# Gaps in SBUF that set where the split moving operands begin against the weights, in a one-core float32 transformer kernel

## The chip, the cores and the metric

One core of one Trainium2 chip runs the whole program in one launch. The metric is device time in microseconds, lower is better. Three runs of the kernel before took 3042.85, 3035.99 and 3043.49 us, median 3042.85.

## The reference, cut to what matters

Two stacks of two layers each work on an activation of 512 tokens by 1024 channels, in float32. The first stack is

```python
x = x + 0.5 * swiglu(rmsnorm(x), w_ffn1_in, w_ffn1_out)     # 1024 -> 2*2816 -> 1024
x = x + mixing_sublayer(rmsnorm(x), ...)                    # retention and forgetting attention, gated
x = x + 0.5 * swiglu(rmsnorm(x), w_ffn2_in, w_ffn2_out)
```

and the second stack runs a hybrid layer twice: one projection of the normed input, four small mixers (window attention, gated convolution, latent attention, stick-breaking attention), group norms, a gate and an output projection. Nearly all arithmetic is a product of the activation with a weight matrix.

## The kernel before

The activation lies channel-major in SBUF as `x`, eight slices of 128 channels by 512 tokens. A float32 product is made from three float32r matmuls: both operands are split into a high part rounded to float32r and the low rest, and the kernel forms high*high + high*low + low*high. The weights come from HBM as 460 panels of 128 x 1024 floats, eight units of 128 columns each. SyncE loads a panel into `raw` (two slots), ScalarE writes its high part to `wh` (L1068), VectorE its low part to `wl` (L1461); `wh` and `wl` have four slots each. The helper `mm3` (L462 to L467) issues for one unit

1. L465: weights `wh` unit, moving high operand (128 x 512 floats),
2. L466: the same weights, moving low operand,
3. L467: weights `wl` unit, moving high operand.

While one matmul streams its moving operand, the weights of the next one are loaded. The moving pairs are `xh`/`xl` (input of every projection of the normed activation, 2384 units), `uh`/`ul` (hidden activation of the feed-forward, 704 units), `mh`/`ml` (128 units), `yrh`/`yrl` and `yfh`/`yfl` (64 each), `ygh`/`ygl` (128) and `cqh`/`cql`, `ckh`/`ckl` (24 in all). In `token_major` (L573 to L575) the roles are exchanged: `xh`/`xl` are the weights, by 128 tokens, and `wh`/`wl` are moving.

Each engine runs its own program, in order, and they meet by semaphores. Of the feed-forward, `ffn_in` runs over 22 pairs of panels with `xh`/`xl` moving, and `ffn_out` over 22 panels with `uh`/`ul` moving; there are four such feed-forwards. In the mixing layer come `token_major` twice, four, then sixteen, then eight panels with `xh`/`xl` between the attention heads, then the merge with `yrh`, `yfh` and `xh` in turn, and the output projection with `mh`/`ml`. The hybrid layer has 25 panels with `xh`/`xl`, one of which (L916 to L919, called the `k_rope` panel here) takes its eight weight blocks not at units of 128 columns but at column 512 + 48*k of the slot, k from 0 to 7.

SBUF tensors are placed one behind the other in the order in which they are declared; each begins at the next multiple of 32 bytes of the partition, and `x` begins at byte 1152. Tensors of a stage that has been closed share their bytes with those of the next. A unit of 128 floats is 512 bytes and a token row of 512 floats is 2048 bytes, so every unit of `wh` and `wl`, and every slice of a moving tensor, has the start of its tensor modulo 512. From the sizes in the code, before the change:

| tensors | start modulo 512 | less the weights' 192 |
| --- | --- | --- |
| `wl`, `wh` | 192 | |
| `xh`, `xl` | 128 | 448 |
| `uh`, `ul`, `yrh`, `yrl`, `yfh`, `yfl`, `mh`, `ml` | 256 | 64 |
| `ygh`, `ygl` | 384 | 192 |
| `cqh`, `cql`, `ckh`, `ckl` | 288 | 96 |
| `ffh` / `ffl` (weights here, one block each 288 bytes) | 224 / 192 | |

The last column is called the distance below: start of the moving operand less start of the weights that are loaded beside it, modulo 512. In `token_major` it is 192 - 128 = 64. In the `k_rope` panel the weights start at 192 + 192*k, so the distance of `xh` to block k is 448 - 192*k: 448, 256, 64, 384, 192, 0, 320, 128 for k = 0 to 7. L465 and L466 of block k stream while weights of the same block are loaded, and L467 while the first of block k + 1 is.

Of the kernel before, what the change touches and what calls it, by code (L numbers as in the profile page):

```python
# [14 lines left out]
F32 = mybir.dt.float32  # L15
# [7 lines left out]
P = 128  # L23
# [120 lines left out]
def build(nc, stream, x_in, vec, const, decay, rope, ff_w, pos, out):  # L144
    ctx = ExitStack()
    with ctx:
        def sb(name, shape, dt=F32, stack=ctx):
            return stack.enter_context(nc.sbuf_tensor(name, shape, dt))

        def sem(name):  # L150
            return ctx.enter_context(nc.semaphore(name))

# [1 line left out]


        x = sb("x", [P, KD, S])
        xh = sb("xh", [P, KD, S], F32R)
        xl = sb("xl", [P, KD, S], F32R)
        sq = sb("sq", [P, S])
# [3 lines left out]
        std_col = sb("std_col", [P, TT])  # L163
        rstd_col = sb("rstd_col", [P, TT])
        raw = sb("raw", [P, RAW_SLOTS, PANEL])
        wl = sb("wl", [P, SLOTS, PANEL], F32R)
        wh = sb("wh", [P, SLOTS, PANEL], F32R)
        vecs = sb("vecs", [P, N_VEC])
# [11 lines left out]


        ffn = ExitStack()
        uh = sb("uh", [P, KF, S], F32R, ffn)
        ul = sb("ul", [P, KF, S], F32R, ffn)
        ta = sb("ta", [P, S], F32, ffn)
# [6 lines left out]
        whole = sb("whole", [P, S], F32, ffn)  # L192
        ffn.close()
        mix = ExitStack()
        yrh = sb("yrh", [P, RH, S], F32R, mix)
        yrl = sb("yrl", [P, RH, S], F32R, mix)
        yfh = sb("yfh", [P, FH // 2, S], F32R, mix)
# [38 lines left out]
        fz, fa = fq[:, 0, :], fq[:, 1, :]  # L236
        heads.close()
        merge_mem = ExitStack()
        mh = sb("mh", [P, KD, S], F32R, merge_mem)
        ml = sb("ml", [P, KD, S], F32R, merge_mem)  # L240
        sr = sb("sr", [P, S], F32, merge_mem)
# [24 lines left out]
        cu = sb("cu", [P, CONV_K - 1 + S], F32, qkv_mem)  # L266
        cy = sb("cy", [P, S], F32, qkv_mem)
        lat_mem = ExitStack()
        cqh = sb("cqh", [P, 2, S], F32R, lat_mem)
        cql = sb("cql", [P, 2, S], F32R, lat_mem)  # L270
        ckh = sb("ckh", [P, S], F32R, lat_mem)
# [27 lines left out]
        out_mem = ExitStack()  # L299
        z = sb("z", [P, KD, S], F32, out_mem)  # L300
        yg = sb("yg", [P, 2, S], F32, out_mem)
        gstd = sb("gstd", [P, 4, TT], F32, out_mem)
        ginv = sb("ginv", [P, 4, TT], F32, out_mem)
        ygh = sb("ygh", [P, KD, S], F32R, out_mem)
        ygl = sb("ygl", [P, KD, S], F32R, out_mem)
        out_mem.close()
        hyb.close()


        raw_in = [sem(f"raw_in{i}") for i in range(RAW_SLOTS)]  # L310
        split_hi, split_lo = sem("split_hi_act"), sem("split_lo_dve")
        panel_done = sem("panel_done")
        x_part = [sem(f"x_part{i}") for i in range(X_PARTS)]
        vec_in, const_in, pos_in = sem("vec_in"), sem("const_in"), sem("pos_in")
# [1992 lines left out]
```

## Time and profile before

| | |
| --- | --- |
| median of three runs | 3042.85 us (3035.99 to 3043.49) |
| time of the profiled execution | 3036.15 us |
| its span, first to last instruction | 3034.4 us |
| TensorE matmul busy | 2953.1 us, 97% of the span |
| weight loads busy | 2378.1 us, 78% |
| VectorE, ScalarE busy | 1446.1 us (48%), 998.1 us (33%) |
| mean granted TensorE clock | 0.989 of full |
| matmuls | 13442 |

Matmuls overlap: a row of the timeline gives 0.39 us for one, while the next starts some 0.23 us behind it. The cost of a matmul in a dense stretch is thus the distance from its start to the next start (called the pitch below), and the duration in the rows is longer than that by the time which the pipeline takes. The page has 40 slices with TensorE at 8 or 9 tenths in each.

### The profile page before, as it was taken

The numbers are of one execution on the slowest core, as the hardware profiler recorded it, in microseconds if no ns is written. First come the engines' busy times: TensorE is split into PE (matmuls) and PEld (weight loads), VectorE is DVE, ScalarE is ACT, GpSimd is POOL, SyncE is SP. The second block draws the span as 40 slices with busy tenths as digits, with TensorE's granted clock in tenths as the row PEclk, the third lists the DMA queues.
The fourth block names the chain that finished last, engine by engine and source line by source line (L and its number), as shares of the span: only waits on it lengthen the run. The fifth ranks groups of instructions, "written<-read, shape, count | busy, mean of one in ns | idle before, by whom it ended". The sixth has DMA issues, their size and how long they took to land.

```text
span 3034.4 us, 36777 instructions
## 1 busy us (share of the span) xinstructions
PE 2953.1 (97%) x13442; PEld 2378.1 (78%) x13442; DVE 1446.1 (48%) x2087; ACT 998.1 (33%) x1546; POOL 0.2 (0%) x4
## 2 busy tenths in 40 slices
PE   8999999999999999999999999999998999999996
PEld 6888887778888887888887778888887877777775
DVE  6443345555544425444255554544435445455555
ACT  3222223333322322222123233332223345434453
POOL 0000000000000000000000000000000000000000
PEclk9999999999999999999999999999999999999998
DMA  4323232212233232323232212323332121122111
GB/s 139 91 89 103 90 115 78 62 56 83 90 97 97 90 104 84 97 91 101 92 116 77 70 55 76 97 84 96 97 98 83 63 69 42 49 84 70 43 42 56
DMA packets 69368, 251.67 MB, mean 83 GB/s; under 512 B 7696, under 2 KB 7824, under 8 KB 69008
## 3 DMA queue, kind: packets, MB, share of 16 engines
q1 hardware_dynamic: 68400, 246.46, 25.8%
q10 hardware_dynamic: 864, 3.79, 0.3%
q8 instruction: 69, 1.13, 0.1%
q14 instruction: 35, 0.29, 0.0%
HBM read 248.13 MB, written 2.10 MB: 82 GB/s over the span
## 4 chain that ended last, share of the span: by engine, by line
PE 93%; DVE 4%; ACT 2%; issue 1%; DMA 0%; DVEq 0%; SPq 0%; ACTq 0%
PE bank L465 26%; PE bank L467 26%; PE bank L466 26%; PE bank L573 1%; PE bank L575 1%; PE bank L574 1%; PE bank L628 1%; PE bank L638 1%; PE bank L818 1%; PE bank L829 1%; PE bank L695 1%; PE bank L804 1%; PE bank L748 1%; PE bank L775 1%; PE bank L760 1%
## 5 line engine op out<-in xcount | busy, mean ns | idle before, releaser
L465 PE MATMUL bank<-xh,wh 128*128 128x512 f32 x2384 | 956.5, 401 | 16.0 <-DVE start_d L2071 9.5
L466 PE MATMUL bank<-xl,wh 128*128 128x512 f32 x2384 | 945.4, 397 | 0.0
L467 PE MATMUL bank<-xh,wl 128*128 128x512 f32 x2384 | 945.0, 396 | 0.0
L1461 DVE TENSOR_TENSOR wl<-raw,wh 128x1024 fp32r<-128x1024 f32 x460 | 561.2, 1221 | 303.6 <-ACT wh L1068 302.9
L1068 ACT ACTIVATE wh<-raw 128x1024 fp32r<-128x1024 f32 x460 | 483.4, 1052 | 398.3 <-PE bank L467 251.9
L465 PEld LDWEIGHTS bank<-xh,wh 128*128 128x128 f32 x2384 | 450.3, 189 | 127.2 <-issue 18.7
L467 PEld LDWEIGHTS bank<-xh,wl 128*128 128x128 f32 x2384 | 449.9, 189 | 109.0
L466 PEld LDWEIGHTS bank<-xl,wh 128*128 128x128 f32 x2384 | 450.3, 189 | 106.5 <-issue 1.9
L1509 DVE TENSOR_TENSOR ta<-bank,rstd 128x512 f32<-128x512 f32 x88 | 60.9, 692 | 463.3 <-PE bank L467 460.7
L467 PE MATMUL bank<-uh,wl 128*128 (+1 forms) x704 | 277.4, 394 | 0.0
L466 PE MATMUL bank<-ul,wh 128*128 (+1 forms) x704 | 276.0, 392 | 0.0
L465 PE MATMUL bank<-uh,wh 128*128 (+1 forms) x704 | 273.2, 388 | 0.0
L1090 ACT ACTIVATE sa<-ta 128x512 f32<-128x512 f32 x88 | 55.8, 634 | 659.8 <-DVE ta L1509 659.7
L466 PEld LDWEIGHTS bank<-ul,wh 128*128 128x128 f32 x704 | 132.2, 188 | 30.9
L465 PEld LDWEIGHTS bank<-uh,wh 128*128 128x128 f32 x704 | 132.2, 188 | 29.6
L467 PEld LDWEIGHTS bank<-uh,wl 128*128 128x128 f32 x704 | 132.4, 188 | 26.3
L573 PE MATMUL bank<-wh,xh 128*128 128x512 f32 (+1 forms) x192 | 75.0, 391 | 6.9 <-DVE xl L1477 6.9
L575 PE MATMUL bank<-wl,xh 128*128 128x512 f32 (+1 forms) x192 | 73.0, 380 | 0.0
L574 PE MATMUL bank<-wh,xl 128*128 128x512 f32 (+1 forms) x192 | 72.7, 379 | 0.0
L1521 DVE TENSOR_TENSOR u<-sa,tb 128x512 f32<-128x512 f32 x88 | 60.9, 692 | 17.8 <-ACT sa L1090 17.8
L465 PE MATMUL bank<-ygh,wh 128*128 128x512 f32 x128 | 53.7, 420 | 7.3 <-DVE ygl L2025 7.3
L1524 DVE TENSOR_TENSOR ul<-u,uh 128x512 f32 (+1 forms) x88 | 60.3, 685 | 0.0
(355 smaller groups left out, 2832.6 us busy)
## 6 DMA issues: line engine op xcount, KB each, us to landing
raw<-stream SPq DMA_DIRECT2D x460, 512.0 KB, 3.5
x<-x_t SPq DMA_DIRECT2D x4, 512.0 KB, 8.1
dec<-decay ACTq DMA_DIRECT2D x2, 1024.0 KB, 6.3
out<-x SPq DMA_DIRECT2D x8, 256.0 KB, 2.0
rp<-rope ACTq DMA_DIRECT2D x2, 512.0 KB, 7.6
cst<-const SPq DMA_DIRECT2D x1, 708.5 KB, 10.8
ffraw<-ff_w ACTq DMA_DIRECT2D x2, 316.0 KB, 9.8
posi<-pos SPq DMA_DIRECT2D x1, 256.0 KB, 10.4
```

The source lines that it names most:

```text
L465: pe.matmul(o, wh[:, s, c], rhs_h, start=first, stop=False)
L466: pe.matmul(o, wh[:, s, c], rhs_l, start=False, stop=False)
L467: return pe.matmul(o, wl[:, s, c], rhs_h, start=False, stop=last)
L573: pe.matmul(o, xh[:, k, tok], wh[:, slot, w], start=k == 0, stop=False)
L574: pe.matmul(o, xl[:, k, tok], wh[:, slot, w], start=False, stop=False)
L575: last = pe.matmul(o, xh[:, k, tok], wl[:, slot, w], start=False, stop=k == KD - 1)
L1068: act.activation(wh[:, at.slot, :], raw[:, at.raw, :], ACT.Copy).then_inc(split_hi, 1)
L1090: act.activation(sa[:], ta[:], ACT.Silu).then_inc(fin_act.sem, 1)
L1461: dve.tensor_tensor(wl[:, at.slot, :], raw[:, at.raw, :], wh[:, at.slot, :].bitcast(F32), ALU.subtract).then_inc(split_lo, 1)
L1509: dve.tensor_tensor(dst, src, rstd[:], ALU.mult).then_inc(st.sem, 1)
L1521: dve.tensor_tensor(u32[:], sa[:], tb[:], ALU.mult).then_inc(fin.sem, 1)
L1524: dve.tensor_tensor(ul[:, j, :], u32[:], uh[:, j, :].bitcast(F32), ALU.subtract)\
```

## The change

A helper `gap` declares a tensor that nothing uses. Seven of them stand ahead of moving operands and of `wl`. No instruction is added, removed or reordered; only addresses differ.

```diff
+        def gap(name, size, stack=ctx):
+            sb("gap_" + name, [P, size // 4], F32, stack)
         x = sb("x", [P, KD, S])
+        gap("xh", 160)
         xh = sb("xh", [P, KD, S], F32R)
...
         raw = sb("raw", [P, RAW_SLOTS, PANEL])
+        gap("wl", 192)
         wl = sb("wl", [P, SLOTS, PANEL], F32R)
...
         ffn = ExitStack()
+        gap("uh", 192, ffn)
         uh = sb("uh", [P, KF, S], F32R, ffn)
...
         mix = ExitStack()
+        gap("yrh", 192, mix)
         yrh = sb("yrh", [P, RH, S], F32R, mix)
...
+        gap("mh", 512, merge_mem)
         mh = sb("mh", [P, KD, S], F32R, merge_mem)
...
+        gap("cqh", 160, lat_mem)
         cqh = sb("cqh", [P, 2, S], F32R, lat_mem)
...
+        gap("ygh", 64, out_mem)
         ygh = sb("ygh", [P, KD, S], F32R, out_mem)
```

By the same arithmetic `wl` and `wh` then begin at 32 modulo 512, and all of `xh`, `xl`, `uh`, `ul`, `yrh`, `yrl`, `yfh`, `yfl`, `mh`, `ml`, `cqh`, `cql`, `ckh`, `ckl`, `ygh` and `ygl` at 288. The distance is 256 for each, and 256 in `token_major` too (32 - 288 modulo 512). Before, `xh`, `uh`, `wl` and `wh` began at multiples of 64 bytes; now they begin 32 bytes past one. The tensors behind `xh` move by 160 bytes and those behind `wl` by 352, those of the mixing layer and the feed-forward by 544; `raw` goes from 192 to 352 modulo 512.

## Rows read from the trace of the kernel before

**Rows 1.** The page: engines, clock by fortieths of the span, chain of work.

```profile
PE 2953.1 (97%) x13442; PEld 2378.1 (78%) x13442; DVE 1446.1 (48%) x2087; ACT 998.1 (33%) x1546; POOL 0.2 (0%) x4
PEclk9999999999999999999999999999999999999998
PE 93%; DVE 4%; ACT 2%; issue 1%; DMA 0%; DVEq 0%; SPq 0%; ACTq 0%
```

**Rows 2.** Waits of TensorE, longest first: who waited for whom, us in total, times, longest.

```profile
PE bank L465 <- DVE start_d L2071: 9.5, 1, 9.5
PE bank L465 <- DVE ygl L2025: 7.3, 8, 2.0
PE bank L489 <- DVE ssq L1488: 7.1, 2, 4.3
```

**Rows 3.** Windows: us, busy us (instructions) of PE, PEld, DVE, ACT, POOL, clock, DMA.

```profile
439.00:687.00 248.00, 242.37 (x1209) 193.64 (x1209) 127.92 (x225) 83.21 (x179) 0.00 (x0) 0.99 0.21 66
687.00:818.00 131.00, 131.00 (x576) 106.95 (x574) 72.77 (x96) 44.41 (x58) 0.00 (x0) 1.00 0.29 93
2345.00:3034.00 689.00, 643.17 (x3147) 511.70 (x3145) 351.69 (x586) 303.57 (x542) 0.00 (x0) 0.97 0.18 57
```

**Rows 4.** Timeline of TensorE in the merge: start us, us, instruction (27, then 24 pitches).

```profile
689.62 0.39 PE L465 MATMUL bank<-yfh,wh 128*128 128x512 f32 x1
...
695.79 0.39 PE L465 MATMUL bank<-xh,wh 128*128 128x512 f32 x1
...
701.38 0.39 PE L465 MATMUL bank<-yrh,wh 128*128 128x512 f32 x1
```

**Rows 5.** Timeline of TensorE in a feed-forward: 27 pitches in `ffn_in`, 27 in `ffn_out`.

```profile
199.69 0.39 PE L465 MATMUL bank<-xh,wh 128*128 128x512 f32 x1
...
205.98 0.40 PE L465 MATMUL bank<-xh,wh 128*128 128x512 f32 x1
...
299.62 0.39 PE L467 MATMUL bank<-uh,wl 128*128 x1
...
305.80 0.39 PE L467 MATMUL bank<-uh,wl 128*128 x1
```

**Rows 6.** Groups, merge and mixing output (690 to 818 us): count, busy us, mean ns of one.

```profile
L467 PE MATMUL bank<-xh,wl 128*128 128x512 f32 x64 | 25.3, 395 | 0.0
L466 PE MATMUL bank<-xl,wh 128*128 128x512 f32 x64 | 25.3, 395 | 0.0
L465 PE MATMUL bank<-xh,wh 128*128 128x512 f32 x64 | 25.3, 395 | 0.0
L467 PE MATMUL bank<-mh,wl 128*128 128x512 f32 x64 | 25.2, 394 | 0.0
L466 PE MATMUL bank<-ml,wh 128*128 128x512 f32 x64 | 25.1, 392 | 0.0
L465 PE MATMUL bank<-mh,wh 128*128 128x512 f32 x64 | 24.8, 388 | 0.0
```

**Rows 7.** Groups in `token_major` (431 to 433 us) and gated output (2640 to 2673).

```profile
L573 PE MATMUL bank<-wh,xh 128*128 128x512 f32 x4 | 1.6, 388 | 0.0
L575 PE MATMUL bank<-wl,xh 128*128 128x512 f32 x3 | 1.2, 394 | 0.0
L574 PE MATMUL bank<-wh,xl 128*128 128x512 f32 x3 | 1.2, 392 | 0.0
...
L466 PE MATMUL bank<-ygl,wh 128*128 128x512 f32 x48 | 19.0, 396 | 0.0
```

**Rows 8.** Groups in 2431.7:2431.9, the `k_rope` panel: exactly its matmuls at distance 256.

```profile
L465 PE MATMUL bank<-xh,wh 128*128 128x512 f32 x1 | 0.4, 393 | 0.0
L466 PE MATMUL bank<-xl,wh 128*128 128x512 f32 x1 | 0.4, 393 | 0.0
L467 PE MATMUL bank<-xh,wl 128*128 128x512 f32 x1 | 0.4, 392 | 0.0
```

**Rows 9.** The same panel at distance 448 (2431.27:2431.30), then at 64 (2770.7:2770.9).

```profile
L466 PE MATMUL bank<-xl,wh 128*128 128x512 f32 x1 | 0.4, 398 | 0.0
L465 PE MATMUL bank<-xh,wh 128*128 128x512 f32 x1 | 0.4, 397 | 0.0
...
L465 PE MATMUL bank<-xh,wh 128*128 128x512 f32 x1 | 0.4, 394 | 0.0
L466 PE MATMUL bank<-xl,wh 128*128 128x512 f32 x1 | 0.4, 388 | 0.0
```

**Rows 10.** Tiles `cqh` and `ffh`: duration ns min/median/max, first and last start, forms.

```profile
L465 PE MATMUL bank<-cqh,wh x16: 394/394/403, 2407.5 to 2750.7; 128*128 128x512 f32 x16
L1844 DVE TENSOR_TENSOR cql<-cn,cqh x4: 685/688/693, 2403.6 to 2743.2; 128x512 fp32r<-128x512 f32 x4
L1040 PE MATMUL bank<-xl,ffh x16: 390/394/403, 433.7 to 1597.0; 128*128 128x512 f32 x16
```

**Rows 11.** A float32 matmul (400 to 420 us), and VectorE's low part of `u` from the page.

```profile
L496 PE MATMUL bank<-diag,cst 128*128 128x512 f32 x2 | 1.0, 590 | 0.0
...
L1524 DVE TENSOR_TENSOR ul<-u,uh 128x512 f32 (+1 forms) x88 | 60.3, 685 | 0.0
```

## The prediction, made before the change was run

> **What bounds the kernel now.** I read the page first. TensorE is busy 97% of the span, 93% of the chain of work lies on it, and its clock is granted in full but for the last slice [rows 1]. Then its waits: the longest total is 9.5 us, at the start, and the next are 7 us each [rows 2]. So what a matmul takes is what the kernel takes, nearly everywhere; the windows show where it isn't so. The merge and the mixing output have no idle time at all (131.00 of 131.00), retention and forgetting attention have 242.37 of 248.00, and only the two hybrid layers leave room, 643.17 of 689.00 [rows 3]. VectorE and ScalarE, at 48% and 33%, stand behind.
>
> **What a matmul costs, by tensor.** The timeline gives starts, and the start is what counts. In the merge, 27 matmuls of `yfh`, `yfl`, `yrh`, `yrl` take 695.79 - 689.62 = 6.17 us, 228.5 ns each, and the 24 of `xh`, `xl` that follow take 701.38 - 695.79 = 5.59 us, 232.9 ns each [rows 4]. In a feed-forward 27 of `xh`, `xl` take 6.29 us, 233.0 ns each, and 27 of `uh`, `ul` 6.18 us, 228.9 ns [rows 5]. The shape and the weights' loading are the same. Stage and load on the other engines differ between the last two, but not between the first two, which stand in one chain without a wait. What differs is which tensor is moving, and so its address: distance 64 for the cheap ones, 448 for `xh`. The durations say the same in whole ns: 388, 392, 394 in turn for `mh`, `ml`, mean 391.3, and 395 for `xh` and `xl` (395.5 by pairs of 393 and 398, which is what the timeline's 0.39 and 0.40 stand for) [rows 6]. Duration less pitch is some 162.5 ns in both, so differences of durations are differences of pitch. `token_major`, with roles exchanged and the distance 64, has 388, 394 and 392, like `mh`; `ygh` at 192 has 396, like `xh` [rows 7]. This is four sets of rows in which one number, the distance, orders the cost.
>
> **What distance 256 costs.** The change puts all these pairs at 256. One panel of the kernel before passes through 256: the `k_rope` panel, whose weight blocks step by 192 bytes. Its three matmuls at 256 last 393, 393 and 392 ns, mean 392.7 [rows 8]. Are single matmuls in passing a fair sample of a steady stretch? The same panel passes 448 with 397 and 398, where the steady value is 395.5, and 64 with 394 and 388, mean 391, where the steady value is 391.3 [rows 9]. So the panel reads within some 2 ns. I take 392.7 for distance 256: 2.8 ns less than `xh` now, 1.4 more than `uh` and its like now.
>
> **The sum, part by part.** The gap ahead of `xh` with the one ahead of `wl` (edits one and two) act on 2384 units of three matmuls, 7152. Of these 4 x 22 x 2 x 24 = 4224 lie in `ffn_in` and 384 in the merge, all on the path. Another 1344 lie between attention heads, where TensorE is busy 98% [rows 3]: I count 9 in 10, 1210. The last 1200, with the 72 of `cqh` and `ckh` (edit six), lie in the hybrid layers, where TensorE waits for heads of other engines; I count half, 636. The 384 of `ygh` (edit seven) are in a dense stretch. Together 6838 matmuls at -2.8 ns, -19.1 us.
>
> The gaps ahead of `uh`, `yrh` and `mh`, together with the move of the weights, act on 704 + 128 + 128 units, 2880 matmuls, and `token_major` has 384 of 512 columns and some 190 of 384 columns, which I count as half: 3360 matmuls, all dense, at +1.4 ns, +4.7 us. The 512 bytes ahead of `mh` change nothing modulo 512 against 0 bytes. Sum: -14.4 us.
>
> Priced at nothing: the tensors that merely move. Float32 matmuls of 512 columns take 590 - 162 = 428 ns, two passes' worth of 214, and show no surcharge that could go [rows 11]; the pairs of them in the hybrid heads move together and keep their distances. VectorE's low part of `cq`, in a tensor at 288 modulo 512 as all will be, takes 685 to 693 ns, and that of `u`, at 256 now, 685 [rows 10, 11]: up to 8 ns dearer, beside matmuls that cover it, on an engine with half its time free. `raw`, whose loads wait for nothing of this, has TensorE's 5.6 us per panel as its cover. If the cover of VectorE were gone, 460 panels at some ns each would be under 4 us.
>
> Of its own profiled time, 3036.15 us, this makes 3021.8. The four times shown of before lie at 3036, 3036, 3043 and 3043, mean 3039.6, and the same spread will stand in the runs of the other kernel. I forecast 3039.6 - 14.4, about 3025 us.
>
> **The rivals.**
>
> *Distance 256 is as good as the best seen, or better.* At distance 64 the steady mean is 391.3, so 4.2 ns off 6838 matmuls, 29 us off: 3011. Were every matmul at 388, the least that recurs [rows 6], it would be 7.5 ns off 6838 and 3.3 ns off 3360, 62 us off: 2978. For it: half a period is the place that looks safest if two readers meet, one at each end. Against it: none of the three rows at 256 is under 392. A variant of the same idea is that the surcharge goes altogether. Then a matmul costs 214 ns, half of the float32 one's 428: 19 ns off 6838 and 15 off 3360, 180 us off, 2860. Rows 8 speak plainly against it, since three in a row at that distance still pay 16; I keep it at one in twenty.
>
> *Slower: the absolute start decides as well.* Before, weights and most moving tensors begin at multiples of 64 bytes; after, all begin 32 past one. Where one of the two does so now, rows are dear: `cqh` at 288 takes 394 at the least and 403 at the most, and `xl` against `ffh`, half of whose blocks lie 32 past, 390 to 403 [rows 10]. If that is a cost of its own and not one of distance, each matmul goes to the 395.5 of `xh` now: nothing gained on `xh`, 4.2 ns lost on 3360, 14 us slower, 3054. At 398, the worst value that recurs, it is 2.5 x 6838 + 6.7 x 3360, 40 us slower, 3079. The point from which it decides is where gain and loss meet: (395.5 x 6838 + 391.3 x 3360) / 10198 = 394.1 ns, only 1.4 above what I take. What speaks against it: where the odd 32 bytes are on one side, the distance is odd too, and the change makes the distance whole again.
>
> *The change does nothing.* The cheap and the dear tensors may differ by higher bits of the address or by the order of the tensors, not by the distance modulo 512. Then 3040, unchanged. Against it, rows 9: within one panel, same tensors, the cost moves as the blocks' starts move by 192 bytes. The Trainium skill has a rule that would give this result: "SBUF — State Buffer", section "Who interferes with whom", gives TensorE two independent read ports, one for the moving operand and one for the loading of weights, and says that it never waits on anyone. By that no placement could matter, and the time would be the same; the trace does not agree, with 228.5 against 232.9 ns in one dense stretch [rows 4].
>
> **How the numbers follow.** My forecast (3012 to 3034) gets 0.42; as good as 64 or better 0.20, the surcharge gone 0.05; unchanged, or gain and loss in balance, 0.14; slower 0.19. The likeliest is 3025. The low end, 2983, takes in nearly all of the first rival; the high end, 3058, its first price of slower, and leaves out the 398 case and the 180 us case, together some 0.13, with a rest of misjudged terms. A difference of 0.3%, 9 us, is about what a measurement of this kernel can tell from none. Forecast and first rival lie under 3030.5 but for the upper part of the forecast's own range: faster 0.62; same 0.20; slower 0.18.
>
> **What would show it.** Right: in the merge and in both halves of a feed-forward the rows of `xh`, `uh`, `mh` and `ygh` become alike, with durations near 392.7 and a pitch near 230 ns, the matmul count, the waits and VectorE's rows unchanged, and the span down by some 14 us, of which the four `ffn_in` give 12. Wrong: `uh` and `mh` at 395 or more (the slower rival), all at 391 or 388 (the first), `xh` still at 395.5 with `mh` at 391.3 (the last). It would be wrong in its size, and not its sense, if passing values at 256 differ from steady ones by more than the 2 ns seen at 448.

## The result, and the profile after

| | before | after |
| --- | --- | --- |
| median of four runs | 3041.45 us (3035.99 to 3043.49) | 2999.86 us (2998.0 to 3005.1) |
| ratio, 95% interval | | 0.987 [0.9855, 0.9885] |
| span of the profiled execution | 3034.4 us | 2997.6 us |
| mean granted clock of the runs (before: thirteen later ones) | 0.986 to 0.990 | 0.981 to 0.984 |

The kernel is 1.3% faster, 41.6 us, where 14.4 had been forecast: the right sign, inside the range, and a gain three times too small. The page after, beside [rows 1]:

```profile
PE 2915.8 (97%) x13442; PEld 2386.8 (80%) x13442; DVE 1446.1 (48%) x2087; ACT 998.0 (33%) x1546; POOL 0.2 (0%) x4
PE 92%; DVE 4%; ACT 2%; issue 1%; DMA 0%; DVEq 0%; SPq 0%; ACTq 0%
```

VectorE is busy for the same 1446.1 us in the same 2087 instructions; only TensorE changed. Lines of the file are 11 further on, so L476 to L478 are what L465 to L467 were. The timeline of the merge, for [rows 4]:

```profile
675.67 0.39 PE L476 MATMUL bank<-yfh,wh 128*128 128x512 f32 x1
...
682.47 0.39 PE L476 MATMUL bank<-xh,wh 128*128 128x512 f32 x1
...
687.91 0.39 PE L476 MATMUL bank<-yrh,wh 128*128 128x512 f32 x1
```

24 matmuls of `xh` and `xl` take 5.44 us, 226.7 ns each, and the 30 from the first `yfh` row to `xh` 6.80 us, 226.7 too. Groups of three dense stretches (count, busy us, mean ns of one) say it in whole ns. They are `ffn_in` at 100 to 250 us, `ffn_out` at 300 to 375 and the mixing output at 680 to 803, beside [rows 6]:

```profile
L476 PE MATMUL bank<-xh,wh 128*128 128x512 f32 x221 | 86.0, 389 | 0.0
L477 PE MATMUL bank<-xl,wh 128*128 128x512 f32 x221 | 86.0, 389 | 0.0
L478 PE MATMUL bank<-xh,wl 128*128 128x512 f32 x221 | 86.0, 389 | 0.0
...
L476 PE MATMUL bank<-uh,wh 128*128 128x512 f32 x41 | 15.9, 389 | 0.0
...
L477 PE MATMUL bank<-ml,wh 128*128 128x512 f32 x64 | 24.9, 389 | 0.0
```

Every family is at 389 ns: 6.5 less than `xh` before, 2.3 less than `uh` and `mh` before, and 3.7 less than the 392.7 that I had taken for distance 256. Duration less 162.3 is the pitch here, 226.7 ns.

Not all of that reached the end. The windows up to the hybrid layers and behind them, of before and then of after (us, busy us of PE, PEld, DVE, ACT, POOL, then clock and DMA):

```profile
0.00:2344.00 2344.00, 2308.93 (x10294) 1865.38 (x10295) 1093.41 (x1501) 693.51 (x1003) 0.20 (x4) 1.00 0.29 91
2344.00:3034.00 690.00, 644.15 (x3148) 512.70 (x3148) 352.69 (x587) 304.57 (x544) 0.00 (x0) 0.97 0.18 57
```

```profile
0.00:2301.00 2301.00, 2266.24 (x10294) 1864.90 (x10294) 1093.38 (x1500) 693.08 (x1003) 0.20 (x4) 1.00 0.30 92
2301.00:2998.00 697.00, 649.57 (x3148) 521.85 (x3148) 352.71 (x588) 304.96 (x544) 0.00 (x0) 0.94 0.18 56
```

The same instruction, the first projection of the hybrid layers, starts at 2344 us before and 2301 after: 43 us won in the first stack. The hybrid layers take 697 us where they took 690: nothing won, 6 or 7 us lost, at a granted clock of 0.94 in place of 0.97.

### The profile page after: what moved, and what is told of

The parts are those of the page before. It is cut to its first block, busy times and chain, and to the rows that moved or that the text cites. A ratio compares the mean times of both kernels' runs of the same rounds, so it can differ in the third digit from the quotient of the medians.

```text
span 2997.6 us, 36777 instructions
## 1 busy us (share of the span) xinstructions
PE 2915.8 (97%) x13442; PEld 2386.8 (80%) x13442; DVE 1446.1 (48%) x2087; ACT 998.0 (33%) x1546; POOL 0.2 (0%) x4
## 4 chain that ended last, share of the span: by engine, by line
PE 92%; DVE 4%; ACT 2%; issue 1%; DMA 0%; DVEq 0%; SPq 0%; ACTq 0%
PE bank L476 25%; PE bank L478 25%; PE bank L477 25%; PE bank L584 1%; PE bank L585 1%; PE bank L586 1%; PE bank L639 1%; PE bank L649 1%; PE bank L829 1%; PE bank L815 1%; PE bank L840 1%; PE bank L706 1%; PE bank L759 1%; PE bank L786 1%; PE bank L771 1%
## 5 line engine op out<-in xcount | busy, mean ns | idle before, releaser
L476 PE MATMUL bank<-xh,wh 128*128 128x512 f32 x2384 | 943.8, 396 | 16.4 <-DVE start_d L2082 9.2
L478 PE MATMUL bank<-xh,wl 128*128 128x512 f32 x2384 | 932.1, 391 | 0.0
L477 PE MATMUL bank<-xl,wh 128*128 128x512 f32 x2384 | 932.0, 391 | 0.0
L476 PEld LDWEIGHTS bank<-xh,wh 128*128 128x128 f32 x2384 | 450.5, 189 | 114.5 <-issue 18.5
L478 PEld LDWEIGHTS bank<-xh,wl 128*128 128x128 f32 x2384 | 450.0, 189 | 95.1
L476 PE MATMUL bank<-uh,wh 128*128 (+1 forms) x704 | 273.9, 389 | 0.0
L478 PE MATMUL bank<-uh,wl 128*128 (+1 forms) x704 | 273.9, 389 | 0.0
L478 PEld LDWEIGHTS bank<-uh,wl 128*128 128x128 f32 x704 | 132.2, 188 | 27.6
L476 PEld LDWEIGHTS bank<-uh,wh 128*128 128x128 f32 x704 | 132.2, 188 | 27.4
L476 PE MATMUL bank<-ygh,wh 128*128 128x512 f32 x128 | 53.9, 421 | 7.0 <-DVE ygl L2036 7.0
```

The lines of the kernel that those rows point to most:

```text
L476: pe.matmul(o, wh[:, s, c], rhs_h, start=first, stop=False)
L477: pe.matmul(o, wh[:, s, c], rhs_l, start=False, stop=False)
L478: return pe.matmul(o, wl[:, s, c], rhs_h, start=False, stop=last)
```

## The experiments

The forecast's price for distance 256 was wrong, and two kernels with other gaps ask by what the pitch is set. All kernels below but the one called `dwell` start from the changed kernel and differ from it in the sizes of the gaps, and where a diff shows it in one thing more; `dwell` starts from the kernel before. Each made one run, but for `even`, `x_only` and `no_mh_gap` with four and `u_only` with ten. "Distance" is again start of the moving tensor less start of `wl` and `wh`, modulo 512. Pitches are means over the dense stretches of a family, from start to next start, gaps over 262 ns left out.

**Two scans of the distance.** One kernel tries several distances, since each family has its own gap (sizes in bytes).

```diff
-gaps: xh 160, wl 192, uh 192, yrh 192, mh 512, cqh 160, ygh 64
+scan_a: xh 416, wl 448, uh 64, yrh 256, mh 64, cqh 128, ygh 480
+scan_b: xh 192, wl 160, uh 160, yrh 480, mh 448, cqh 320, ygh 160
```

> The gaps are resized so that each family of moving tensors has a distance of its own to wl and wh: xh/xl 0, uh/ul 128, yrh/yfh 320, mh 384, ygh 160, cqh 224 (and 0 for token_major). Theory D (the distance modulo 512 sets the pitch, and 256 is the bottom of it): xh at 0 is the dearest, at 235 ns or more, the others between, and the span goes up to 3040 us or over. Rival P (the period is 256, since 448 and 192, which are 256 apart, cost the same before): xh at 0 costs what 256 does, 226.7 ns, and mh at 384 what uh at 128 does; the span is near 3000 us. Rival A (the absolute start, 32 past a multiple of 64 for both operands, gave the gain): xh, uh and mh, all still 32 past, keep 226.7 and ygh, now at a multiple of 64, does not.

> As the scan before, with the distances xh/xl 288, uh/ul 224, yrh/yfh 32, mh 480, ygh 352, cqh 416 (and 224 for token_major). Theory D: xh and uh, 32 bytes to either side of 256, stay within 2 ns of 226.7 if the optimum is broad, or go to 230 and over if it is narrow; yrh and mh, next to 0, are dear. Rival P: 32 and 288 cost the same, and so do 224 and 480. Rival A: all of xh, uh, yrh, mh at multiples of 64 while the weights are 32 past; all dear, 231 to 240.

The first ran in 3009.5 us, the second in 3050.9. Groups in `ffn_in` and `ffn_out` of the first (`xh` at 0, `uh` at 128), then of the second (288 and 224):

```profile
L476 PE MATMUL bank<-xh,wh 128*128 128x512 f32 x221 | 86.0, 389 | 0.0
...
L476 PE MATMUL bank<-uh,wh 128*128 128x512 f32 x36 | 14.2, 395 | 0.0
```

```profile
L476 PE MATMUL bank<-xh,wh 128*128 128x512 f32 x215 | 85.0, 395 | 0.0
...
L476 PE MATMUL bank<-uh,wh 128*128 128x512 f32 x28 | 11.1, 396 | 0.0
```

With the two kernels already known, this is the whole scale at steps of 32 bytes:

| distance | pitch, ns | distance | pitch, ns |
| --- | --- | --- | --- |
| 0 | 227.3 (`xh`, scan_a) | 256 | 226.7 to 227.1 (after) |
| 32 | 233.3 (`yrh`, scan_b) | 288 | 233.3 (`xh`, scan_b) |
| 64 | 228.9 (`uh`, before) | 320 | 229.0 to 230.1 (`yfh`, `yrh`, scan_a) |
| 96 | 233.9 (`cqh`, before) | 352 | 233.3 (`ygh`, scan_b) |
| 128 | 233.3 (`uh`, scan_a) | 384 | 232.4 (`mh`, scan_a) |
| 160 | 234.2 (`ygh`, scan_a) | 416 | 234.3 (`cqh`, scan_b) |
| 192 | 233.3 (`ygh`, before) | 448 | 233.3 (`xh`, before) |
| 224 | 233.3 (`uh`, scan_b) | 480 | 233.3 (`mh`, scan_b) |

The right half repeats the left, within 1.2 ns. So rival P stands: the period is 256, and distance 0 is as good as 256. It isn't that two readers should start half a period apart; being at the same place in the period is the good case. Most distances cost the same 233.3, and two places, 0 and 64 modulo 256, are better.

**The absolute start.** Both sides moved by 160 bytes, to multiples of 64.

```diff
-gap("xh", 160)
+gap("xh", 320)
...
-gap("mh", 512, merge_mem)
```

> All distances 256 as in the changed kernel, but weights and moving tensors begin at multiples of 64 bytes (wl, wh at 192 modulo 512, the moving ones at 448), as they did before the change. Theory D: 226.7 ns for every family, time as the changed kernel, 2998 to 3005 us, ratio to before 0.987. Rival A (the 32 bytes past a multiple of 64 matter): the gain is lost at least in part, pitch 229 to 233, time 3020 to 3045 us.

3002.8 us (2999.6 to 3004.0), ratio 0.9875 [0.9856, 0.9893], and 389 ns for `xh`, `uh` and `mh` alike. The absolute start, at 32 past a multiple of 64 or at one, doesn't matter at distance 256. It doesn't at 64 either: `uh` has 228.9 ns with starts of 256 against weights at 192 (before) and of 96 against 32 (`x_only`, below). Rival A, in the prediction as the slower case, has fallen.

**Steps of less than 32 bytes.** Each tensor 512 bytes longer, and read from an offset:

```diff
-        xh = sb("xh", [P, KD, S], F32R)
+        xh = sb("xh", [P, KD * S + P], F32R)[:, 4:4 + KD * S].rearrange("p (a b) -> p a b", b=S)
...
-        mh = sb("mh", [P, KD, S], F32R, merge_mem)
+        mh = sb("mh", [P, KD * S + P], F32R, merge_mem)[:, 1:1 + KD * S].rearrange("p (a b) -> p a b", b=S)
```

(`xl` and `ml` likewise, and `uh`, `ul` from element 124, which puts them at distance 240 modulo 256).

> The changed kernel with the moving tensors shifted by less than 32 bytes: xh and xl at distance 272, uh and ul at 240, mh and ml at 260. If 256 is a point on a slope, one of 272 and 240 is cheaper than 226.7 ns and the other dearer; if it is the bottom of a narrow well, both are dearer, 228 to 233.3, and 260 between; if only the 32-byte block of the address counts, 272 and 260 stay at 226.7 and 240 goes to 233.3, as 224 does.

3047.2 us. In the mixing output and merge of this kernel `mh` is at 260, `xh` at 272 and `yfh` at 256:

```profile
L476 PE MATMUL bank<-mh,wh 128*128 128x512 f32 x52 | 20.8, 401 | 0.0
...
L476 PE MATMUL bank<-xh,wh 128*128 128x512 f32 x48 | 18.9, 394 | 0.0
L478 PE MATMUL bank<-yfh,wl 128*128 128x512 f32 x31 | 12.1, 389 | 0.0
```

Four bytes beside the good place cost 11 ns more per matmul (mean 238.0 against 226.7), 16 bytes 5 ns (231.7), and `uh`, 16 bytes to the other side, 9 ns (235.8). So 256 isn't a point on a slope, and the 32-byte block of the address isn't all that counts. But the expectation, that 260 would lie between 256 and its neighbours, missed: the nearest is the dearest. Two of the three, 235.8 and 238.0, are dearer than every multiple of 32 in the table; 231.7 isn't. The weights stayed at a multiple of 32 here, so these three rows don't tell the distance from the moving tensor's own start being off a multiple of 32; moving the weights by the same 4 bytes would, and wasn't tried.

**What my price was read from.** The kernel before, own addresses, with one edit that keeps the whole `k_rope` panel at distance 256. It reads other weight columns there, and so leaves out the rope part of the keys.

```diff
-                    c = KR_AT + k * KR_W
+                    c = KR_AT + KR_W + (k % 3) * P
```

> The kernel before, with its own addresses, but in the k_rope panel the weight blocks begin at column 560, 688 or 816 of the slot in turn, which keeps all 24 matmuls of the panel at distance 256 (it reads other weight columns, so the rope part of the keys is left out in effect). This is the row that my price for 256 was read from, three matmuls long, made 24 long. Theory S (a stretch needs some ten matmuls to settle, and my three were read on the way): the first seven to twelve vary between 224 and 236 ns, then all are 226 or 227. Rival A (a matmul at 256 in the old layout really costs 230 to 231, and the changed kernel gained by its absolute addresses): the mean stays at 230 to 231 to the end of the panel. Outside the panel nothing changes, time within 8 us of before.

3041.2 us, as before. The panel begins in the second hybrid layer at 2769.27 us. Its second to sixth matmul (window 2769.67:2770.62), and then fifteen in a row from 2771.1 on:

```profile
L467 PE MATMUL bank<-xh,wl 128*128 128x512 f32 x2 | 0.8, 396 | 0.0
L466 PE MATMUL bank<-xl,wh 128*128 128x512 f32 x2 | 0.8, 394 | 0.0
L465 PE MATMUL bank<-xh,wh 128*128 128x512 f32 x1 | 0.4, 389 | 0.0
...
L466 PE MATMUL bank<-xl,wh 128*128 128x512 f32 x5 | 1.9, 389 | 0.0
L467 PE MATMUL bank<-xh,wl 128*128 128x512 f32 x5 | 1.9, 389 | 0.0
L465 PE MATMUL bank<-xh,wh 128*128 128x512 f32 x5 | 1.9, 389 | 0.0
```

One by one the durations are 394, 393, 398, 389, 395, 393 and then 389 for every matmul. The panel of the first hybrid layer gives the same seven values in the same order, and then 389. The old addresses give 389 as soon as the stretch is long enough. The same shows at the head of each dense stretch of the changed kernel: pitches of 230, 236, 229, 232, 231 and then 227, 226, 227 without end; the longest such heads are nine or ten matmuls. So a matmul's pitch depends on what ran before it, and not on its distance alone. My three matmuls at 256 [rows 8] followed others at 448, and were on the way.

**Whose weights count.** With 192 bytes between `wl` and `wh` the distance is no longer the same for the two.

```diff
-        gap("wl", 192)
         wl = sb("wl", [P, SLOTS, PANEL], F32R)
+        gap("wh", 192)
         wh = sb("wh", [P, SLOTS, PANEL], F32R)
```

(and the gaps ahead of `xh`, `mh` and `ygh` resized, for the distances that the expectation names).

> A gap of 192 bytes between wl and wh, so that the two have different distances. xh, uh, yrh: 256 to wh and 448 to wl; mh: 64 to wh, 256 to wl; ygh: 384 to wh, 64 to wl. If the distance counts to the weights that are being loaded for the next matmul, the second of each three (it streams while wl is loaded) is the odd one: for xh and uh its pitch is 231 or more and the first and the third are near 227. If the distance to the matmul's own weights counts, the third is the odd one. If only the moving operand's address counts, all three are alike. Mean of xh between 227 and 233 in either case of the first two, span 3005 to 3025 us.

3041.3 us, not the 3005 to 3025 expected. `xh` in `ffn_in`:

```profile
L478 PE MATMUL bank<-xh,wl 128*128 128x512 f32 x217 | 86.3, 397 | 0.0
L477 PE MATMUL bank<-xl,wh 128*128 128x512 f32 x217 | 85.1, 392 | 0.0
L476 PE MATMUL bank<-xh,wh 128*128 128x512 f32 x217 | 84.4, 389 | 0.0
```

The third is the odd one, so I could have read this as "own weights count". But the mean, 231.1, is that of two dear matmuls (233.3) and one cheap (226.7), not of one dear. Two more kernels were made for that. The first leaves the weights and moves the low operand (`xl`, `ul`) to 448:

> The changed kernel, but a gap of 192 bytes between xh and xl and between uh and ul, so that the low operand, which the second of each three matmuls streams, is at 448 and the high one at 256. This tells which matmul a surcharge is booked to: if to the streaming one itself, the second of three is the odd one for xh and uh, at 233 or more. If it shows one matmul later, the third is the odd one; then the kernel with wl and wh apart, where the third was the odd one, speaks of the weights that are loaded while the second streams and not of the third's own. Mean of xh 229 to 233, span 3015 to 3035 us.

```profile
L477 PE MATMUL bank<-xl,wh 128*128 128x512 f32 x219 | 85.8, 392 | 0.0
L476 PE MATMUL bank<-xh,wh 128*128 128x512 f32 x219 | 85.4, 390 | 0.0
L478 PE MATMUL bank<-xh,wl 128*128 128x512 f32 x219 | 85.2, 389 | 0.0
```

3018.7 us, as expected, but no single odd one at 233: the surcharge is spread over the three (229.2, 229.2, 228.3 for `uh`), with a mean of 228.9, which is one dear and two cheap. So the mean counts dear matmuls and the booking to one of the three says little. The second puts every moving tensor at 256 to `wl` and at 448 to `wh` (`gap("wh", 320)`):

> wh 320 bytes further from wl: every moving tensor is at 256 to wl and at 448 to wh (before, in the first such kernel, it was 448 to wl and 256 to wh, and the mean was 231.1 ns, which is two of three matmuls at 233.3 and one at 226.7). If the distance to the matmul's own weights or to the ones being loaded each makes it dear, all three of a unit are dear now: mean 233.3. If only one of the two counts, two of three are dear and the mean is 231.1.

3058.3 us; `xh` 233.0, `uh` and `mh` 233.3: all three dear. Own weights alone would make the first and the second dear, the loaded ones alone the first and the third. Together with the first kernel (own 256, loaded 448: the second of three; own 448, loaded 256: the third; and two dear in the mean) this fits a rule that a matmul is cheap only when both its own weights and the next ones lie well. Two more families of the first kernel fit it: `mh`, 64 to `wh` and 256 to `wl`, has the 228.9 of distance 64 (229.1 measured), and `ygh`, 384 and 64, has all three dear (233.3). But the rule rests on means, and two families don't fit: with the same distances in the last kernel, `cqh` settled at 231.1 and `ygh` at 232.2, which I can't explain. Nor is "own weights" told from another reading of the same rows: that a load at a bad distance is dear, and so is a matmul whose weights and the next ones begin at different places.

**Is it the loading at all?** The second of each three with half of its weights:

```diff
-                pe.matmul(o, wh[:, s, c], rhs_l, start=False, stop=False)
+                half = slice(c.start, c.start + P // 2)
+                pe.matmul(o[0:P // 2], wh[:, s, half], rhs_l, start=False, stop=False)
```

> The changed kernel with the second matmul of each three on 64 of its 128 weight columns (half of the high times low product is left out), so that one load of three reads 256 bytes instead of 512. Theory L (what is left above 213 ns, 13.3 ns, is still the price of loading weights beside the stream): the mean pitch falls by 2 to 5 ns, some matmul of the three to 220 or less. Rival F (226.7 ns is what streaming 512 float32r columns costs, loading or not): all three stay at 226.7. Rival N (the shorter load breaks the settled pattern): the mean goes up.

3018.2 us. (This kernel leaves out half of the product of high weights and low operand.) The mean goes up to 229.8 in every family (229.87 `xh`, 229.78 `uh` and `mh`), which is rival N: no pitch stays at 226.7, and in its place fifteen pitches between 224 and 236 repeat, 231, 236, 228, 233, 230, 226 and so on, the values of an unsettled head. Theory L, that the mean falls, and rival F, that nothing changes, have fallen. That it is the shorter load isn't shown, since the same edit also halves the rows that the matmul writes. It doesn't answer either how much of the 12.7 ns above 214 (half of a float32 matmul, [rows 11]) is the loading's; no settled pitch lies under 226.7, though single ones fall to 223 or 224.

**One part at a time,** with the gap of 512 bytes left out in a third kernel.

```diff
 x_only: xh 160, wl 192, cqh 160, ygh 64          (uh, yrh, yfh, mh stay at 64)
 u_only: uh 192, yrh 192                          (all else as before)
 no_mh_gap: as the change, less the 512 ahead of mh
```

> Only the gaps ahead of xh and wl (and cqh, ygh), so xh, xl, cqh, ckh and ygh are at 256, while uh, yrh, yfh and mh stay at 64. By the settled pitches of the changed kernel and the one before (xh 233.3 to 227.1, uh and its like 228.9 as before) it keeps the 37 us that xh gives in the first block and lacks 2.2 ns x 2880 = 6.3 us of the changed kernel: 3004 to 3010 us. Rival (the parts aren't additive, since TensorE's clock in the hybrid layers follows from how the work falls in time): the first block is 6 us longer than in the changed kernel, 2307 us, but the hybrid layers differ by up to 10 us either way.

> Only the gaps ahead of uh and yrh: uh, yrh, yfh and mh at 256, xh at 448 and the rest as before. Worth 2.2 ns x 2880 = 6.3 us by settled pitches, nothing by my price for 256, which had it dearer by 4 us: 3034 to 3037 us against 3045, at a median of 3041 for before. Ratio 0.997 to 0.999.

> The changed kernel without the 512 bytes ahead of mh. All distances and all starts modulo 512 are the same. Expected the same pitches, 226.7 ns for mh, and a time of 2998 to 3005 us. It gives more executions of the changed kernel's layout for the clock in the hybrid layers: by the theory that quicker matmuls leave TensorE more waiting there, the mean granted clock stays at 0.981 to 0.985 in all of them, against 0.986 to 0.990 before; if that was chance, it will show 0.986 and over in about half of them.

| | median, us | ratio to before | clock of the runs | first stack in the profiled one |
| --- | --- | --- | --- | --- |
| before | 3041.1 (13 runs) | | 0.986 to 0.990 | 2344.0 |
| x_only | 3003.9 | 0.9888 [0.9861, 0.9916] | 0.981 to 0.987 | 2309.7 |
| u_only | 3038.6 (10 runs) | 0.9999 [0.9988, 1.001] | 0.985 to 0.987 | 2338.4 |
| no_mh_gap | 3000.7 | 0.9867 [0.9847, 0.9888] | 0.981 to 0.985 | 2302.9 |

In the first stack the parts nearly add up: 34.3 from `xh`, 5.6 from `uh` and its like, 39.9 against 42.7 together (41.1 in `no_mh_gap`), each from one execution. `x_only` came out at the lower edge of the 3004 to 3010 expected. At the end of the kernel the 5.6 us of `u_only` can't be told from nothing, and my expectation of 0.997 to 0.999 missed. The windows of its profiled execution show where they stayed:

```profile
0.00:2338.00 2338.00, 2303.24 (x10294) 1865.04 (x10294) 1093.13 (x1500) 692.70 (x1003) 0.20 (x4) 1.00 0.29 91
2338.00:3041.00 703.00, 656.62 (x3148) 520.47 (x3148) 353.18 (x588) 304.90 (x545) 0.00 (x0) 0.95 0.18 56
```

Its hybrid layers have the old distances and the old matmuls of `xh`, and take 703 us instead of 690, at a clock of 0.95 instead of 0.97. (13 us is more than typical, since this execution, 3043.0 us, is among the slowest of its ten, and the profiled one of before, 3036.15, in the faster half of its kernel's.) The clock has two levels, 2.4 GHz and half of it, and the traces record how long each held. From the start of the hybrid layers to the end:

| | hybrid layers, us | of these at 1.2 GHz, us (stretches) | estimate, us |
| --- | --- | --- | --- |
| before | 690.3 | 46.9 (6) | |
| u_only | 702.8 | 70.7 (8) | 702.2 |
| x_only | 691.8 | 67.2 (8) | 692.0 |
| after | 696.3 | 80.0 (10) | 698.4 |
| even | 700.5 | 87.7 (11) | 702.2 |
| no_mh_gap | 702.0 | 91.3 (12) | 704.0 |

The estimate is worked out from these rows: the 690.3 of before, plus half of what was added at 1.2 GHz, less 8.5 us for the quicker matmuls where `xh` is at 256. (Those at full speed there went from 233.2 to 228.0 ns, 1129 of `xh`, and from 233.3 to 226.9, 342 of `ygh`, with 48 of `cqh` 7.2 ns less.) It meets all five within 2.1 us. So the hybrid layers' length in these kernels is told by the pitch and the time at half clock; why that time differs isn't. In the twelve executions of the change's layout (four of the change, four of `even`, four of `no_mh_gap`) the whole kernel's clock was 0.981 to 0.985, in the thirteen of before 0.986 to 0.990, without overlap; chance, the rival that `no_mh_gap` was to test, would hardly do that. But the ten of `u_only`, whose `xh` has the old pitch, lie across the two, at 0.985 to 0.987. Within each kernel too the longer runs are those with the lower clock: 2994.5 us at 0.985 and 3006.7 at 0.981 for `no_mh_gap`, 3033.9 at 0.990 and 3043.9 at 0.986 for before.

## Why the prediction was right or wrong

**What bounds the kernel: right.** TensorE's pitch is the kernel's time in the first stack. 5952 matmuls of `xh` there at 6.2 ns less (233.3 to 227.1, unsettled heads included) are 37 us, 3264 of the others at 2.2 ns less 7 us, together 44; 42.7 were measured in the two profiled executions.

**That distance decides: right, for a reason that was half right.** Four sets of rows ordered by one number were four samples of a function that has only a few values. The experiments confirm the number, with a period of 256 and not 512: that 448 and 192 cost the same and 256 apart was in my own rows [rows 6, 7], and I did not follow it. It would have said that 256 is like 0.

**The price for 256: wrong, the step that failed.** I took 392.7 ns from three matmuls in passing; the settled value is 389. I had asked whether passing matmuls are a fair sample, and answered with the means at 448 and 64 [rows 9]. That check couldn't find the fault. At 64 the settled state is itself a round of 388, 392, 394, and an unsettled stretch has similar values, so the two agree by chance; at 448 the alternation of 393 and 398 hid it likewise. The three rows at 256, each 3 to 4 ns above the value at which they would have settled, looked the steadiest of all. With 389 in its place, the same sum is 6.5 x 6838 + 2.3 x 3360 = 52 us, where 14.4 was forecast and 41.6 measured. That 3000 us lay inside the range is owed to the range, which took in the first rival, and not to the price.

**The sign for `uh` and its like: wrong with it.** +4.7 us was forecast; the first stack of `u_only` shows -5.6.

**The hybrid layers: wrong the other way.** I counted half of their matmuls as gained. Their matmuls at full speed did get shorter, by some 8.5 us in sum, but the layers took 6 us longer, since the clock stood at 1.2 GHz for 80.0 us in place of 46.9. I had named the clock as granted in full but for the last slice; a digit of 9 there means 90% or more, and my own row for these layers had 0.97 [rows 3]. I priced nothing for a clock that falls further. Of the 52 us, 10 are missing in the medians, and 15 between the two profiled executions (36.8 won).

**The rivals.** "As good as the best seen, or better" was the case that came: its variant with 388 for all had nearly the right price, 389. Its reason, that half a period is the safest place, was wrong, for 256 is a whole period and as good as 0. I gave it 0.20 with the sentence that none of the three rows is under 392, which was true and no argument. The surcharge did not go altogether. The slower rival, absolute starts 32 bytes past 64, was tested alone and fell. "The change does nothing" fell. The Trainium skill, "SBUF — State Buffer", section "Who interferes with whom", says that TensorE never waits on anyone. What I drew from it, that no placement could matter, doesn't hold: distances of 256 and 288 differ by 6.6 ns per matmul. Why the placement costs anything is not shown by this. For the pitch, the Trainium skill's "TensorE: Matmul & The Clock Gate", section "Wait — 56ns, not 53.3ns?", gives 215.7 ns for 512 columns back to back; the best settled pitch here, with float32r operands and a load beside every matmul, is 226.7, and no float32r matmul of this case reached that figure.

**The gap of 512 bytes:** nothing, as said; 3000.7 against 2999.9 us.

**What stays open:** why 0 and 64 modulo 256 are good, what sets the 13 ns that remain above 214, what a start off a multiple of 32 bytes costs by itself, and whether the lower clock in the hybrid layers is bound to the shorter matmuls or to how the work falls in time. `u_only` had more time at half clock with the old matmuls there; `scan_a`, with `xh` at 227.3 ns as well, had a clock of 0.987 in its one run, and `x_only` ranged from 0.981 to 0.987.

## What to carry to other kernels

When a matmul's pitch differs between tensors of one shape in one dense stretch, look at the starts of the moving operand and the weights: put all of them, `wl` and `wh` too, at the same place modulo 256 bytes. The three starts off a multiple of 32 that were tried cost 5 to 11 ns each. Read the price of a condition only from rows where it has lasted a dozen matmuls; a check of passing rows against a settled value is worth something only where settled and unsettled values differ. And a gain on TensorE counted in full here only where it had no idle time; where it had, the granted clock took it back, so look at the clock before and after.

## What was not expected of the hardware

- Mean pitches of float32r matmuls with 512 columns are few: 226.7, 228.9, 231.1 and 233.3 ns cover most dense stretches. (Others met were 229.8, 231.7, 232.3, 234.2, 235.8 and 238.0.) Multiplied by three they are 680, 687, 693 and 700, steps of 6.7.
- Less work made the stream slower: one matmul in three with half of its weight columns, +3 ns per matmul in the mean (226.7 to 229.8).
- The same matmuls in the hybrid layers took 690 or 703 us, with 47 or 71 us of it at half clock, when only tensors of the first stack had moved (one execution each).
- Four bytes of offset cost 11 ns per matmul, 5%, on a tensor that is otherwise unchanged; sixteen cost 5 or 9.
